# Score products on padded heads in the mixers, the norm table ahead of the others, and compressed keys and values in four units between query units

## What is computed

```python
# first block: compressed keys and values, per head of 64 channels, four heads
chunks = kv.reshape(B, T // 16, 16, G, D)
blocks = concatenate([chunks[:, :-1], chunks[:, 1:]], axis=2) + pos[None, None, :, None, :]
hid = gelu(einsum('bnlgd,ldf->bngf', blocks, w1) + b1)
out = einsum('bngf,fd->bngd', hid, w2) + b2
...
# second block, for each of two layers: four mixers on the split projection
pa, pb, pc, pd = split(rms_norm(x, mix_norm) @ w_in)
ya = neighbourhood_mixer(pa, ...)   # 4 heads of 64, each query tile on 256 keys, with a bias
yb = mla_mixer(pb, ...)             # 4 heads of 96, dense
yc = diff_mixer(pc, ...)            # 4 heads x 2 maps of 32, dense, with a bias
yd = gqa_mixer(pd, ...)             # 4 query heads on 2 key heads of 64, dense
```

## Time and profile before

| | us |
|---|---|
| runs | 3602.8, 3612.03, 3619.43 |
| median | 3612.03 |
| profiled execution | 3616.18, its span 3614.1 |

### The profile page before, as it was taken

One profiled execution on the slowest core, in us unless ns is written; L12 is line 12 of the kernel. 1 busy time (PEld: TensorE's weight loads), 2 busy tenths in 40 slices (PEclk: granted clock), 3 DMA queues, 4 the chain that ended last, 5 costly groups with the idle time before them and its releaser, 6 DMA issues.

```text
span 3614.1 us, 41572 instructions
## 1 busy us (share of the span) xinstructions
PE 3373.2 (93%) x15430; PEld 2684.8 (74%) x15430; DVE 1743.0 (48%) x2598; ACT 1313.3 (36%) x1861; POOL 206.2 (6%) x220
## 2 busy tenths in 40 slices
PE   6978988999999999999888999999999988979998
PEld 4657876788888888866377788888886647968887
DVE  5444458445553455333564555445543355455542
ACT  2224646223333333222256333333322223643332
POOL 1010110001000000000110100010000011010000
PEclk8977999999999999999788999999999976989999
DMA  4330012333333333332132233333333213213332
GB/s 104 82 91 4 1 30 70 82 94 93 99 97 92 97 93 99 90 97 70 45 87 54 82 97 99 86 99 96 97 92 97 70 46 72 68 54 106 96 92 66
DMA packets 535406, 287.71 MB, mean 80 GB/s; under 512 B 57225, under 2 KB 521931, under 8 KB 535142
## 3 DMA queue, kind: packets, MB, share of 16 engines
q1 hardware_dynamic: 530596, 275.49, 27.8%
q0 software_dynamic: 3040, 9.65, 0.8%
q10 hardware_dynamic: 1634, 0.72, 0.1%
HBM read 264.80 MB, written 2.14 MB: 74 GB/s over the span
## 4 chain that ended last, share of the span: by engine, by line
PE 86%; DVE 7%; ACT 2%; issue 2%; SPq 1%; DMA 1%; POOL 1%; DVEq 0%; POOLq 0%; ACTq 0%; PEldq 0%
PE bank L376 23%; PE bank L378 23%; PE bank L377 23%; PE bank L994 5%; PE bank L975 4%; PE bank L983 3%; SPq L1985 1%; PE bank L886 1%; PE bank L687 1%; PE bank L794 1%; DVE wlo L352 1%; PE bank L1519 1%; DVE both L749 1%; ACT whi L345 0%; DVE xc L1726 0%
## 5 line engine op out<-in xcount | busy, mean ns | idle before, releaser
L376 PE MATMUL bank<-hhi,whi 128*128 128x512 f32 x2560 | 1015.3, 397 | 37.5 <-DVEq L416 25.7
L378 PE MATMUL bank<-hlo,whi 128*128 128x512 f32 x2560 | 1002.0, 391 | 0.0
L377 PE MATMUL bank<-hhi,wlo 128*128 128x512 f32 x2560 | 1002.0, 391 | 0.0
L352 DVE TENSOR_TENSOR wlo<-raw,whi 128x1024 fp32r<-128x1024 f32 x489 | 612.1, 1254 | 611.6 <-ACT whi L345 603.0
L345 ACT CAST whi<-raw 128x1024 fp32r<-128x1024 f32 x489 | 509.4, 1046 | 440.0 <-PE bank L378 419.5
L376 PEld LDWEIGHTS bank<-hhi,whi 128*128 128x128 f32 x2560 | 482.8, 189 | 189.2 <-issue 89.0
L377 PEld LDWEIGHTS bank<-hhi,wlo 128*128 128x128 f32 x2560 | 482.9, 189 | 103.7 <-issue 4.3
L378 PEld LDWEIGHTS bank<-hlo,whi 128*128 128x128 f32 x2560 | 482.1, 188 | 104.3 <-issue 0.5
L378 PE MATMUL bank<-ulo,whi 128*128 128x512 f32 x880 | 350.3, 398 | 0.0
L377 PE MATMUL bank<-uhi,wlo 128*128 128x512 f32 x880 | 347.0, 394 | 0.0
L376 PE MATMUL bank<-uhi,whi 128*128 128x512 f32 x880 | 346.1, 393 | 0.0
(11 more groups left out here) (400 smaller groups left out, 3579.8 us busy)
## 6 DMA issues: line engine op xcount, KB each, us to landing
raw<-in_ffn_w_gate SPq DMA_DIRECT2D x88, 512.0 KB, 4.0
raw<-in_ffn_w_up SPq DMA_DIRECT2D x88, 512.0 KB, 3.8
raw<-in_w_in SPq DMA_DIRECT2D x74, 512.0 KB, 3.8
raw<-in_ffn_w_down SPq DMA_DIRECT2D x64, 512.0 KB, 3.9
raw<-in_w_out SPq DMA_DIRECT2D x24, 512.0 KB, 3.9
raw<-in_ffn_w_down SPq DMA_DIRECT2D x32, 384.0 KB, 3.4
raw<-in_w_gate SPq DMA_DIRECT2D x22, 512.0 KB, 4.0
raw<-in_w_up SPq DMA_DIRECT2D x22, 512.0 KB, 3.8
```

The costliest lines, as they stand in the source:

```text
L352: k.nc.vector.tensor_tensor(k.wlo[:, slot, :], k.raw[:, slot, :], k.whi[:, slot, :].bitcast(F32), ALU.subtract)\
L376: mm(out, whi, hi(kc), start=start and kc == 0, stop=False)
L377: mm(out, wlo, hi(kc), start=False, stop=False)
L378: last = mm(out, whi, lo(kc), start=False, stop=stop and kc == kcs - 1)
```

## The change

**Compressed keys and values.** Four chunks of two heads each take the place of the eight duplicated ones, each followed by a query chunk; four more query chunks follow. That is 21 chunks. `add_positions` makes both heads' halves from one chunk, in eight additions, half of which read one half of the partitions and write the other; a second copy of the positions with the halves exchanged (`swapped`, four small copies) serves these. The low parts (two a chunk) are now made ahead of the next additions.

```diff
     m = rows_by_chunk(w["w_in"][0])
-    for b in range(2):
-        for g in range(NG):
-            halves(m, O_KV + b * KV + g * HD, O_KV + b * KV + g * HD)
-    for gp in range(2):
-        for hh in range(HPG):
-            halves(m, (2 * gp * HPG + hh) * HD, ((2 * gp + 1) * HPG + hh) * HD)
+    for c in range(KC):
+        if c < 4:
+            block(m, 0, KC, O_KV + c * P, P)
+        first = 2 * (c // HPG) * HPG + c % HPG
+        halves(m, first * HD, (first + HPG) * HD)
...
+            for h, (both, _, _) in enumerate(chunks[c]["blocks"]):
+                head = slice(HD * h, HD * h + HD)
+                tokens = chunks[c]["dest"].rearrange("p (n i e) -> p e i n", i=CMP_S // 2, e=2)[head]
+                for v in range(2):
                     at = v * CMP_S // 2
-                    last = nc.vector.tensor_tensor(both[rows, at:at + CMP_S // 2, :], tokens,
-                                                   spread(pos[rows, at:at + CMP_S // 2], 32), ALU.add)
+                    for e in range(2):
+                        pos = chunks[c]["positions"][0 if e == h else 1][head, at:at + CMP_S // 2]
+                        last = nc.vector.tensor_tensor(both[HD * e:HD * e + HD, at:at + CMP_S // 2, :], tokens[:, e],
+                                                       spread(pos, 32), ALU.add)
...
+            if c - 1 in blocked:
+                low(c - 1)
             if c in blocked:
                 add_positions(c)
-            if c - 1 in blocked:
-                low(c - 1)
```

```diff
+                    pool.dma_start(into[:, :, :], k.consts["into2"]).then_inc(*k.into_landed.up(by=16))
                     for v in (vA, vB, vC, vD):
                         pool.memset(v[:, :, :, HD], 1.0).then_inc(*k.q_zero.up())
-                    pool.dma_start(into[:, :, :], k.consts["into2"]).then_inc(*k.stage_landed.up(by=16))
...
-                k.stage_ready = k.stage_landed.all()
+                k.stage_ready = k.into_landed.all()
...
             for i in beside(c):
                 if i == 0:
+                    pe.wait_ge(*tables_ready)
                     pe.wait_ge(*k.rn_ready.at(2))
```

```diff
-        for u in range(4, 14):
-            part, v = (0, u - 4) if u < 8 else (1, u - 8) if u < 12 else (2, u - 12)
-            sp.wait_ge(*k.parted.at((1 + v // 2) if u < 8 else (3 + v // 2) if u < 12 else 6))
+        for u in range(10, 14):
+            v = u - 10
+            sp.wait_ge(*k.parted.at(1 + v // 2))
             sp.wait_ge(*k.qk_done.at(ends[u - 2]))
...
+        if t in (5, 9):
+            c = (t - 5) // 4
+            parts([(kA[:, c, :], *near_keys[c])], k.keys_split)
+        if t in (8, 12, 16, 20):
+            h = (t - 8) // 4
+            dve.wait_ge(*k.qk_done.at(ends[2 + h]))
+            r = 64 * (h % 2)
+            parts([(qA[r:r + 64, h // 2, :], slot[h % 2][0][r:r + 64], slot[h % 2][1][r:r + 64])], k.padded)
...
+    def three(rows, hi, lo, keys):
+        return [(x[:, rows], key) for x, key in ((hi, keys[0]), (hi, keys[1]), (lo, keys[0]))]
```

More of the change, by code:

```diff
@@ L970, in scores @@
                 pe.wait_ge(*(k.exp_done if steps[t - 4]["bias"] is None else k.low_done).at(t - 3))
-            if ready and t in ready:
-                pe.wait_ge(*ready[t])
+            for sem, value in ready.get(t, ()) if ready else ():
+                pe.wait_ge(sem, value)
             pairs = steps[t]["pairs"]
@@ L1261, in first_projection, with _ @@
     k.stage_ready = k.stage_landed.all()
-    pos = [vector(k, "cmp_pos_k"), vector(k, "cmp_pos_v")]
-    chunks = [dict(rows=P, dest=tmp[:, g % 2, :], blocks=(both[:, g % 2, :, :], dhi[b][:, :, :, g], dlo[b][:, :, :, g], pos[b]))
-              for b in range(2) for g in range(NG)]
-    chunks += [dict(rows=P, dest=raw_queries(otok, c), norm=c) for c in range(KC)]
+    pos, swapped = [vector(k, "cmp_pos_k"), vector(k, "cmp_pos_v")], sb("swapped", [P, 2, 16])
+    @k.block.vector
+    def _(dve):
+        for b in range(2):
+            for e in range(2):
+                nc.vector.tensor_copy(swapped[64 * e:64 * e + 64, b, :], pos[b][64 - 64 * e:P - 64 * e, 0:16])\
+                    .then_inc(*k.small_ready.up())
+        dve.wait_ge(*k.small_ready.all())
+    chunks = []
+    for c in range(KC):
+        if c < 4:
+            b, g = c // 2, 2 * (c % 2)
+            chunks.append(dict(rows=P, dest=tmp[:, c % 2, :], positions=(pos[b], swapped[:, b, :]),
+                               blocks=[(both[:, h, :, :], dhi[b][:, :, :, g + h], dlo[b][:, :, :, g + h])
+                                       for h in range(2)]))
+        chunks.append(dict(rows=P, dest=raw_queries(otok, c), norm=c))
     chunks += [dict(rows=P, dest=kT[:, c, :], norm=KC + c) for c in range(4)]
@@ L1908, in mix @@
                               for c in range(2)]
-                    project(k, chunks, into, NORM2_HEADS, (items, back, scales))
+                    project(k, chunks, into, NORM2_HEADS, (items, back, scales, k.stage_landed.all()))
                     handover(k)
@@ L1937, in mix, with mixers @@
         handover(k, pe_waits=False)
-def mixers(k, mem, l, near, latent, diff, shared, lam, ytok):
+def mixers(k, mem, l, near, latent, diff, shared, parted, lam, ytok):
     nc = k.nc
@@ L2012, in latent_head, with parts @@
+    def splits(dve, t):
+        def parts(trios, done):
+            for src, hi, lo in trios:
+                last = nc.vector.tensor_copy(hi, src)
+            last.then_inc(*k.part_hi.up())
+            dve.wait_ge(*k.part_hi.all())
+            for src, hi, lo in trios:
+                last = nc.vector.tensor_tensor(lo, src, hi.bitcast(F32), ALU.subtract)
+            last.then_inc(*done.up())
         def latent_head(h):
             hi, lo, khi, klo = (x[0:MD] for x in slot[h % 2])
-            nc.vector.tensor_copy(hi, qB[0:MD, h, :])
@@ L2068, in mixers @@
         groups.append(dict(steps=heads, out=ytok[:, :, h * 64:h * 64 + 64], add=False, factor=None))
+    for v in range(2):
+        for j in range(2):
+            h = 2 * v + j
+            groups.append(dict(steps=[dict(pairs=three(slice(u * P, (u + 1) * P), *slot[v][2 * j:2 * j + 2], shared_keys),
+                                           width=T, bias=None, values=[vD[:, t, v, :] for t in range(TB)])
+                                      for u in range(TB)],
+                               out=ytok[:, :, 3 * GW + h * 64:3 * GW + h * 64 + 64], add=False, factor=None))
     for h in range(4):
```

153 lines of the change are left out of this document (71 added, 82 removed).

## The result

The changed kernel takes 3571.3 us (median of 4 runs, 3564.1 to 3581.9), the kernel before beside it 3615.7 us (4 runs, 3602.8 to 3621.7): a ratio of 0.9884, 95% interval 0.9845 to 0.9923, some 44 us. The forecast was 3555 us, range 3536 to 3578. Sign and cause hold, two of three terms hold in size, and the time is 16 us above the forecast. Of these, 4.9 us lie between the two profiled executions: they went from 3616.2 to 3564.1 us, 52.1 where I had 57. The other 11.4 us are how far a profiled execution lies from the median: the new one is 7.2 us under its own, and I had taken off 4.2 us because the old one lay above its own.

A forecast was written before the change was run, and what follows sets the result against it. TensorE, busy for 93% of the span, was taken to bound the kernel. From the profiled 3616.2 us, first projection -25, norm table -14 and mixers -18 gave 3559.2, less 4.2 for the median: 3555 us, range 3536 to 3578.

The forecast's parts named there:

- First projection, -25: First projection: four units of products, a 2.96 us wait and a restart go, VectorE falls slightly behind; 25 us less.
- that rival: First projection: additions crossing between partition halves take twice 0.60 us, giving 3574 us; chance 0.06.
- Norm table, -14: Second blocks' projection: TensorE no longer waits for the last table, 5.5 and 5.2 us, plus restarts 3.0; 14 us less.
- Mixers, -9 per layer: Mixers: 16.7 us of standing and low clock go, 5.4 of products and 2.5 of VectorE's lag come; -18 in both.
- third products: Mixers' near and shared steps: one added product each, 5.4 us per layer, all on TensorE's path.
- VectorE's lag: Mixers, 16th to 32nd step: VectorE's extra splits cost 2.5 us per layer, bounds 0 and 6.
- the two zeroings: Mixers: GpSimd's zeroings beside VectorE's splits were taken to cost 0, bounds 0 and 2 us.
- The clock, one layer low and one not: Mixers' latent heads: one layer keeps its 34 us stretch at 1.2 GHz; without it the sum is 17 us lower.
- My sign of being wrong: VectorE's pair well above 13 us, waits for pads above 6 us, or low clock in stretches that had none.
- The rival of both layers at full clock: Mixers' latent heads: neither layer has the low-clock stretch, giving 3538 us; chance 0.17.
- Late copies: Mixers' difference heads: two units of each layer still wait for copies, 25 us, giving 3580 us; chance 0.08.
- the clock low after the near heads: Mixers' 48 shared and difference steps at 1.2 GHz: 150 us more in both layers, 3705 us; chance 0.02.

The follow-up runs named there:

- e1_projection: The kernel before with the new first projection alone (four compressed units between query units): 3579.6 us, ratio 0.9931 to before.
- e5_two_products: The changed kernel with the third product of each near and shared score left out, so part of the computation is missing: 3546.3 us, ratio 0.984 to before.
- e3_mixers: The kernel before with the new mixers alone (padded near and shared heads, shared heads ahead of difference heads): 3595.0 us, ratio 0.997 to before.
- e6_bias_late: The changed kernel with each zeroing in eight pieces and GpSimd's twelve bias tables started after VectorE's fourth latent split: 3537.5 us, ratio 0.9819 to before.

## Why the prediction was right, and where it was not

- **What bounds the kernel: right.** All that was gained came from TensorE: products gone, waits gone, clock kept.
- **First projection, -25: right.** 25.7 in the profile, 26.6 and, by the time, 24 in e1_projection. Products, wait and restart went as written. VectorE's pair is 12.5 us, not 12.8, and the crossing additions cost 0.59 us: that rival falls.
- **Norm table, -14: right.** 6.3 and 6.8 us, 13.1 in all. From the last product to the resumed one it is 3.22 us instead of 8.67 in the first layer, 5.45, where I had 5.5, and 3.14 instead of 8.34 in the second, 5.20, where I had 5.2. The restart I had put at 1.5 us in each layer. In the first it stayed (8.11 us to the next norm product, after 8.72, 0.6 gained), in the second it went (6.61 after 9.53, 2.9 gained). The two sum to 3.5 us where I had 3.0; that one layer made up for the other is luck. The stage as a whole gained less in the second layer (6.8 us) than these two pieces (8.1), which no row explains.
- **Mixers, -9 per layer: right in kind, the size failed.** No wait on a copy is left, near steps take 1.03 us after 0.90, shared steps 2.03 us against 2.02 forecast. The cuts above give, per layer in the mean (six layers with the old mixers, four with the new): length 143.8 to 138.2 us, -5.6; idle time 11.8 to 5.3, -6.5; busy 132.0 to 132.9, +0.9. At full clock the third products add 5.3 us of busy time (e5_two_products), so the clock gave back 4.4.

| term, per layer | forecast | measured |
|---|---|---|
| idle of TensorE, with VectorE's lag | -10.7 + 2.5 = -8.2 | -6.5 |
| clock lost in it | -6.0 | -4.4, all causes |
| third products | +5.4 | +5.3 |
| sum | -8.8 | -5.6 |

The term that failed is the one I had put at 0, the two zeroings beside VectorE's splits, with 2 us as the far bound. In the four layers of after and e3_mixers TensorE stood behind a zeroing for 1.45, 1.74 and 1.45 us and not at all in the fourth, and 10, 17 and 7 us at low clock followed: 1.2 us of standing and, at half speed, about 4.3 us of clock per layer. The clock of the copies I had read in one of the two layers that lost least: by the granted clock in slices of 2 us, 17 us at low clock around and behind the copies there, 17 to 34 in the six old layers, 26 in the mean. What went there was thus more than I had forecast, and it hides part of the zeroings' price in the sum. VectorE's lag was the other way, about 1.5 us per layer where I had 2.5.

The page SBUF — State Buffer of the Trainium skill (Who interferes with whom) says that a copy or cast of VectorE can run in a mode that takes a pair of ports shared with GpSimd, that whoever issues first has the pair for the whole instruction and the other one is blocked, and that a VectorE instruction with two operands in SBUF contends only with a GpSimd instruction that reads. The rows agree. The cast takes 2.10 us beside the zeroing's 1.80, though its record starts 0.02 us ahead. A subtraction that runs inside the other zeroing of that layer takes its usual 0.68 us:

```profile
2981.97 2.08 POOL L2011 MEMSET hhi<- 64x2048 f32 x1 [3.27 <-PE bank L978]
```

```profile
2982.34 0.68 DVE L2045 TENSOR_TENSOR hhi<-qA,hhi 64x512 fp32r<-64x512 f32 x1
```

Beside the bias additions, which read, both kinds are stretched. The trace of before had rows for such a price, and I had not read them: the fourth head's split took 3.6 us beside the bias tables.

- **The clock, one layer low and one not: right for the profile, wrong as a fixed term.** After has one such stretch, in the other layer. It is a matter of each layer of each execution, at a price of 13 to 17 us, behind a wait that I had seen as harmless. My sign of being wrong, low clock in stretches that had none, did come: this stretch, and the 10 us behind the zeroing. So did a miss on the length: cut as in the earlier trace rows, the first layer takes 156 us where I had 143, and the second 149 after 169.5. The rival of both layers at full clock had 3538 us, and e6_bias_late takes 3537.5; it shows both layers at full clock, but it is another kernel with two more edits, and the equal number is chance. The row of 28.00 us busy at 0.52 speaks, as the earlier trace rows did, against the rule of the Trainium skill (TensorE: Matmul & The Clock Gate, Part 1: The HAM clock gate) that sustained activity lifts the throttling.
- **Late copies, and the clock low after the near heads:** neither came. No wait on a copy stands in either layer, and the steps from 3012 to 3106 us are at full clock.

That the measured time lies inside the range owes something to chance as well: the mixers gained 11 us in the mean and not 18, and profile and median differ by 4 to 7 us in either direction.

Left open: why the same wait of 2 us brings the low clock in one layer and not in the next, and what other clock the executions lose outside the mixers, where the profiles of after and e6_bias_late differ by 5.4 us ahead of the second blocks' projection, with the same instructions. The ten profiles with the new first projection fall into two groups there: five reach that projection at 1570 to 1571 us, five at 1575 to 1577.

## What to carry to other kernels

Price what two engines do side by side, not only on one: a split on VectorE beside work of GpSimd, off the critical path by every total, made TensorE stand for 1.5 to 2 us, and the low clock that came behind it in some layers cost several times as much. When a term rests on waits and on the clock behind them, read it in every layer and in more than one profile before it enters a sum. And where a part is worth less than the spread of the runs, cut the trace at fixed marks: the norm table, lost in 50 us of spread, shows there as 6 to 7 us per layer.

## What was not expected of the hardware

- A standing of TensorE of 2.05 us in otherwise dense work was followed by 27 us at 1.2 GHz with TensorE busy for all of it (27.00 of 27.00 us at 0.52) in one layer and not in the other; 1.45 us alone was not in two layers.
- VectorE's cast of 64x512 took 2.10 us beside one zeroing of 64x2048 by GpSimd, 0.61 us beside eight of 64x256, and 0.42 us alone; in pieces the zeroing itself took 2.36 us against 1.80.
- The same gap of TensorE, 3.1 to 3.4 us behind the first products of a projection, was followed by a restart at low clock in ten of ten first layers and in two of ten second layers.
- An addition that reads 64 partitions and writes the other 64 took the 0.59 us of one in place.
